# An encoder trunk on one core: the first block's rounding moved to VectorE, the first transfers reordered, fewer warm-up products, second block ordered by operand

## The chip, the cores and the metric

The kernel runs on one core of one Trainium2 chip. The metric is the device time of one execution in microseconds (us), as the median of several runs. One further execution was recorded by the hardware profiler; every row below comes from that one. PE is TensorE, PEld its weight loads, DVE is VectorE, ACT is ScalarE, POOL is GpSimd and SP is SyncE, which here only starts transfers.

## The reference, cut to what matters

Two layers work on a sequence of 512 tokens with 1024 features, all in float32. Each layer adds a token mixer (in layer 0 a short gated convolution, in layer 1 a two-dimensional neighbourhood attention) and then a squared-ReLU MLP to `x`. Only the very first steps are touched by the change:

```python
h = rmsnorm(x, norm_mix[0])
u = h @ conv_w_in[0]          # 1024 x 3072
gate_b, gate_c, v = jnp.split(u, 3, axis=-1)
```

where `rmsnorm(x, g) = x * rsqrt(mean(x*x) + eps) * g`. The kernel multiplies `x` by the gain `g` before the product and by the reciprocal root after it, so the product can start before any mean is known.

## The kernel before, in words

**Precision.** Every float32 operand is split in two parts of a reduced format (float32r): a high part, which is the value rounded, and a low part, which is the value less the high part. A product is then three matmuls that add into the same PSUM bank: high times high, high times low and low times high. For `x` the high part is `a_h` and the low part `a_l`; for weights these are `wave_h` and `wave_l`, views of `w_h` and `w_l`.

**The start.** `x` lies transposed (features on partitions) and comes as eight blocks of 128 features by 512 tokens, `xT[:, k, :]`, 256 KB each, a part of the tile `big`. The first wave of weights is the first four units of `conv_w_in` (four slices `s` of 128 output columns), again in eight blocks by feature: `wave[k]` is 256 KB and lands in `raw`. `par` holds the norm gains and the convolution taps, 32 KB.

- SP starts `par` (L568), then in turn `x[0]`, `x[1]`, `wave[1]`, `x[2]`, `wave[2]` and so on (L570, L572), then four transfers of `x` in token order (`xs`, L574) and the ring of later weights (L592). All of it is one queue, q1.
- ACT starts `wave[0]` itself (L1319), on its own queue q10. It then loads its function table (L1321), rounds `wave[0]` into `wave_h` (L1323, semaphore `piece_hi`), waits for `par`, and rounds in turn `x[k]` times its gain into `a_h` (L1327, semaphore `a_hi`) and `wave[k]` into `wave_h` (L1330).
- DVE waits for `par`, subtracts to get `wave_l` of block 0 (L1824, `piece_split`), and then in turn makes `a_l` (L1828, `a_ready`) and `wave_l` (L1836) of each block.
- PE first runs eight float32 warm-up products of 128 columns on constants (L996); each shows as two passes. POOL makes those constants. Then come the twelve matmuls of block 0, ordered by operand: four slices of high times high (L1001), four of `wave_l` (L1004), four of `a_l` (L1007), each group behind its own semaphore. For blocks 1 to 7 PE waits for `a_ready` and `piece_split` (from block 4 on `w_split`) of that block and runs the twelve matmuls slice by slice through the helper `three` (L769, L770, L771).

After block 7 the remaining units of `conv_w_in` follow, 24 matmuls each. From unit 8 on PE waits for `taken`: DVE must have taken the result of eight units earlier out of its bank (L1819), for which it needs the reciprocal root, computed by ACT and DVE from `xs` and spread over the partitions by two transfers that POOL starts. All later stages (the rest of the convolution, both MLPs, the attention, the final norm) are untouched.

Of the kernel before, what the change touches and what calls it, by code (L numbers as in the profile page):

```python
# [7 lines left out]
KT = D // P  # L8
# [110 lines left out]
def part_end(s, name):  # L119

    return MATRIX[s][0] + 2 * MATRIX[s][1].index(name) + 2
# [99 lines left out]
def encoder(nc, x, x_tok, wave, weights, blocks, sevens, small, gains, rpb, out):  # L221
    f32, f32r = mybir.dt.float32, mybir.dt.float32r
    ALU, ACT = mybir.AluOpType, mybir.ActivationFunctionType
    ctx = ExitStack()
    with ctx:
# [3 lines left out]
        def sem(name):  # L229
            return ctx.enter_context(nc.semaphore(name))  # L230

        xs = sb("xs", [P, 4, D])
        a_h = sb("a_h", [P, KT, SEQ], f32r)
        a_l = sb("a_l", [P, KT, SEQ], f32r)
# [7 lines left out]
        par = sb("par", [P, 8 * KT])  # L242
# [8 lines left out]
        wave_h = wh_all.rearrange("p s (k n) -> p s k n", k=KT)  # L251
        wave_l = wl_all.rearrange("p s (k n) -> p s k n", k=KT)

        def stage(k):
            return raw_all[:, 4 * P * k:4 * P * (k + 1)].rearrange("p (s n) -> p s n", s=4)
# [39 lines left out]
        xT = hraw  # L295
# [71 lines left out]
        bank = [banks[:, 512 * b:512 * b + 512] for b in range(8)]  # L367
# [47 lines left out]
        first_in = [sem(f"first_in{k}") for k in range(KT)]  # L415
        x_in = [sem(f"x_in{m}") for m in range(KT)]
        xs_in = sem("xs_in")
        par_in = sem("par_in")
# [18 lines left out]
        piece_hi = sem("piece_hi")  # L437
        piece_split = sem("piece_split")
        half_hi = sem("half_hi")
        wave_done = sem("wave_done")  # L440
        w_hi = sem("w_hi")
# [10 lines left out]
        rstd_out = sem("rstd_out")  # L452
        rstd_in = sem("rstd_in")
        a_hi = sem("a_hi")
        a_ready = sem("a_ready")

        h_ready = sem("h_ready")
# [62 lines left out]
        def gain(n, m):  # L520
            return par[:, n * KT + m:n * KT + m + 1]
# [43 lines left out]

        @block.sync
        def _(sp):
            sp.dma_start(par[:], small).then_inc(par_in, 16)  # L568
            for k in range(KT):
                sp.dma_start(xT[:, k, :], x[k]).then_inc(x_in[k], 16)  # L570
                if k:
                    sp.dma_start(raw_all[:, 4 * P * k:4 * P * (k + 1)], wave[k]).then_inc(first_in[k], 16)  # L572
            for t in range(4):
                sp.dma_start(xs[:, t, :], x_tok[t]).then_inc(xs_in, 16)  # L574

            plain = [w for w in UNIT_OF_RING if part_of(w) is None]

            def ring_source(r):

                w = UNIT_OF_RING[r]  # L580
                if part_of(w) is None:
                    return weights[plain.index(w)]
                i, part, u = part_of(w)
                at = slice(D * u, D * u + D)
                return sevens[i, Y_ROLES.index(part)][:, at] if part in Y_ROLES else t_dram[i][int(part[1]) - 1][:, at]

            def load_ring(first, last):
                for r in range(first, last):
                    sp.wait_ge(w_split, UNIT_OF_RING[r - 4] + 1)
                    if UNIT_OF_RING[r] in (W_V, W_WO):  # L590
                        sp.wait_ge(t_made[0 if UNIT_OF_RING[r] == W_V else 1], 16 * 4)
                    sp.dma_start(raw_all[:, D * (r % 4):D * (r % 4 + 1)], ring_source(r)).then_inc(raw_in[r % 4], 16)  # L592

            def load_matrix(q, roles=LOAD_ORDER):

                before = {at: role for role, at in ROOMS[q - 1].items()}
                for role in roles:
                    was = before[ROOMS[q][role]]
                    if q == SEQ_ATTN:
                        sp.wait_ge(pv_done, 2 * KT)  # L600
                        sp.wait_ge(s_lo["S4"], 2)
                    elif was != "free":
                        sp.wait_ge(w_split, part_end(q - 1, LAST_USE[was]))
                    elif q in (2, SEQ_ATTN + 1):
                        sp.wait_ge(x_lo, 19 * by_unit(1 if q == 2 else CHUNKS + 1) + 16)
                    else:
                        sp.wait_ge(w_split, part_end(q - 2, "P4"))
                    if was == "T2" and q != SEQ_ATTN:
                        sp.wait_ge(t3_in, 16 * q)
                        sp.wait_ge(t4_in, 16 * q)  # L610
                    sp.dma_start(room[ROOMS[q][role]], blocks[q, Y_ROLES.index(role)]).then_inc(y_in[role], 16)

            load_ring(4, W_OUT + 4)
            load_matrix(1)
            load_ring(W_OUT + 4, W_OUT + 8)
            for q in range(2, SEQ_ATTN):
                load_matrix(q)
            sp.wait_ge(unit_done, MATRIX[SEQ_ATTN - 1][0])
            ends = [ring_of(W_MLP1) + i for i in (-2, 0, 1, 3, 8)]
            load_ring(W_OUT + 8, ends[0])  # L620
            for i, role in enumerate(LOAD_ORDER):
                load_matrix(SEQ_ATTN, (role,))
                load_ring(ends[i], ends[i + 1])
            for q in range(SEQ_ATTN + 1, N_MATRIX):
                load_matrix(q)
            sp.wait_ge(out_act, 1)
            sp.dma_start(out[1], xn[1]).then_inc(stored, 16)
            sp.wait_ge(out_act, 2)
            sp.dma_start(out[0], xn[0]).then_inc(stored, 16)
            sp.wait_ge(out_act, 3)  # L630
            sp.dma_start(out[2][:, 512:D], xn[2][:, 512:D]).then_inc(stored, 16)
            for t in (2, 3):
                sp.wait_ge(out_ready, t - 1)
                sp.dma_start(out[t][:, 0:512], xn[t][:, 0:512]).then_inc(stored, 16)
            sp.wait_ge(stored, 16 * 5)
# [130 lines left out]
        def _(pe):  # L766
# [225 lines left out]
                        last.then_inc(unit_done, 1)  # L992

            pe.wait_ge(const_ready, 3)
            for _ in range(8):
                nc.tensor.matmul(bank[5][:, 0:P], ones[:], ident[:], start=True, stop=True)  # L996

            pe.wait_ge(piece_hi, 1)
            pe.wait_ge(a_hi, 1)
            for s in range(4):  # L1000
                nc.tensor.matmul(bank[s][:], wave_h[:, s, 0, :], a_h[:, 0, :], start=True, stop=False)  # L1001
            pe.wait_ge(piece_split, 1)
# [2 lines left out]
            pe.wait_ge(a_ready, 1)  # L1005
            for s in range(4):
                nc.tensor.matmul(bank[s][:], wave_h[:, s, 0, :], a_l[:, 0, :], start=False, stop=False)  # L1007
            for k in range(1, KT):
                pe.wait_ge(a_ready, k + 1)
                if k < 4:  # L1010
                    pe.wait_ge(piece_split, k + 1)
                else:
                    pe.wait_ge(w_split, k - 3)
                for s in range(4):
                    last = three(bank[s][:], wave_h[:, s, k, :], wave_l[:, s, k, :], a_h[:, k, :], a_l[:, k, :],
                                 False, k == KT - 1)
                    if k == KT - 1:
                        last.then_inc(unit_done, 1)
                if k == 4:
                    last.then_inc(wave_done, 1)  # L1020
# [87 lines left out]
        def _(act):  # L1108
# [208 lines left out]
                    second(tc + c)  # L1317

            act.dma_start(raw_all[:, 0:4 * P], wave[0]).then_inc(first_in[0], 16)  # L1319
            act.wait_ge(const_ready, 1)  # L1320
            nc.scalar.activation(tok[:, 4, :], ones[:, 0:4], ACT.Sqrt)  # L1321
            act.wait_ge(first_in[0], 16)
            nc.scalar.activation(wave_h[:, :, 0, :], stage(0), ACT.Copy).then_inc(piece_hi, 1)  # L1323
            act.wait_ge(par_in, 16)
            for k in range(KT):
                act.wait_ge(x_in[k], 16)
                nc.scalar.activation(a_h[:, k, :], xT[:, k, :], ACT.Copy, scale=gain(0, k)).then_inc(a_hi, 1)  # L1327
                if k:
                    act.wait_ge(first_in[k], 16)
                    nc.scalar.activation(wave_h[:, :, k, :], stage(k), ACT.Copy).then_inc(piece_hi if k < 4 else w_hi, 1)  # L1330

            act.wait_ge(xs_in, 16 * 4)
            for t in range(4):
# [159 lines left out]
        def _(dve):  # L1493
# [323 lines left out]
            def scaled(w, b, dst):  # L1817
# [1 line left out]
                nc.vector.tensor_tensor(dst, bank[b][:], rstd, ALU.mult).then_inc(taken, 1)  # L1819

            dve.wait_ge(par_in, 16)

            dve.wait_ge(piece_hi, 1)
            nc.vector.tensor_tensor(wave_l[:, :, 0, :], stage(0), wave_h[:, :, 0, :].bitcast(f32), ALU.subtract  # L1824
                                    ).then_inc(piece_split, 1)
            for k in range(KT):
                dve.wait_ge(a_hi, k + 1)
                nc.vector.scalar_tensor_tensor(out=a_l[:, k, :], in0=xT[:, k, :], scalar=gain(0, k),  # L1828
                                               in1=a_h[:, k, :].bitcast(f32), op0=ALU.mult,
                                               op1=ALU.subtract).then_inc(a_ready, 1)  # L1830
                if k:
                    if k < 4:
                        dve.wait_ge(piece_hi, k + 1)
                    else:
                        dve.wait_ge(w_hi, k - 3)
                    nc.vector.tensor_tensor(wave_l[:, :, k, :], stage(k), wave_h[:, :, k, :].bitcast(f32), ALU.subtract  # L1836
                                            ).then_inc(piece_split if k < 4 else w_split, 1)
# [348 lines left out]
```

## Time and profile before

| | us |
|---|---|
| median of three runs | 1039.65 |
| lowest and highest of them | 1038.97, 1040.02 |
| the profiled execution, its own time | 1039.44 |
| its span, first to last instruction | 1037.3 |
| PE busy in it | 1028.6 (99%) |
| DVE, ACT, POOL busy | 842.0 (81%), 599.2 (58%), 105.1 (10%) |

The span leaves 2.1 us of the execution's time outside the first and last instruction. Times of rows are from the start of the span. In a timeline row the columns are start, duration, engine, line, operation, what is written and read with its shape, and the number of instructions merged; in brackets stands the idle time of that engine before it and what ended it. A matmul's duration is longer than the distance between two of them, since they are pipelined, and their ends are modelled.

### The profile page before, as it was taken

What the parts mean: (1) busy time and instruction counts of PE and PEld (TensorE: products, weight loads), DVE (VectorE), ACT (ScalarE), POOL (GpSimd) and SP (SyncE); (2) the same over time, 40 slices, a digit from 0 to 9 for tenths busy, and PEclk for the clock granted to TensorE, in tenths of its full rate; (3) what the DMA queues carried; (4) which work ended last, traced back from release to release, by engine and by line L of the source; (5) the groups of instructions that cost most, each with busy time, mean ns of one, the idle gap of its engine ahead of it and who ended that gap; (6) DMA issues with size and microseconds to landing.
All of it is one profiled execution on the core that took longest, in us unless ns stands there. A gap on an engine that the chain in (4) does not pass through costs nothing.

```text
span 1037.3 us, 15366 instructions
## 1 busy us (share of the span) xinstructions
PE 1028.6 (99%) x6088; PEld 903.3 (87%) x6088; DVE 842.0 (81%) x1173; ACT 599.2 (58%) x837; POOL 105.1 (10%) x160
## 2 busy tenths in 40 slices
PE   9999999999999999999999999999999999999997
PEld 7888888988998998998888888889888988988985
DVE  4497788699899689688997667797899798698697
ACT  6221356565584574575775555656664774674675
POOL 0347101000000000001013000000000000000003
PEclk9999999999999999999999999999999999999999
DMA  8798979226745645633998733166056547447423
GB/s 325 141 397 288 292 204 251 84 50 224 205 131 163 186 130 172 175 99 97 372 263 238 212 106 111 43 213 253 1 127 208 163 133 202 149 134 202 148 51 112
DMA packets 37110, 182.97 MB, mean 176 GB/s; under 512 B 5808, under 2 KB 5936, under 8 KB 22960
## 3 DMA queue, kind: packets, MB, share of 16 engines
q1 hardware_dynamic: 23184, 108.57, 29.8%
q0 software_dynamic: 13568, 72.91, 28.4%
q8 instruction: 48, 0.79, 0.3%
q10 hardware_dynamic: 288, 0.52, 0.2%
q14 instruction: 22, 0.18, 0.1%
HBM read 137.20 MB, written 27.33 MB: 159 GB/s over the span
## 4 chain that ended last, share of the span: by engine, by line
PE 95%; DVE 3%; DMA 1%; ACT 1%; issue 0%; POOL 0%; POOLq 0%; ACTq 0%; DVEq 0%
PE bank L769 30%; PE bank L770 30%; PE bank L771 30%; PE bank L974 2%; PE bank L952 1%; PE bank L937 1%; DVE w_l L1508 1%; DMA raw<-weights 1%; PE bank L792 1%; DVE big L1947 0%; PE bank L996 0%; DVE hx L1953 0%; DVE a_l L1721 0%; ACT big L1167 0%; ACT big L1144 0%
## 5 line engine op out<-in xcount | busy, mean ns | idle before, releaser
L1116 ACT ACTIVATE w_h<-big 128x1024 fp32r<-128x1024 f32 x210 | 221.7, 1058 | 216.2 <-PE bank L771 215.5
L769 PE MATMUL bank<-a_h,w_h 128*128 128x256 f32 (+1 forms) x892 | 294.4, 330 | 0.3 <-DVE w_l L1508 0.3
L771 PE MATMUL bank<-a_h,w_l 128*128 128x256 f32 (+1 forms) x892 | 292.8, 328 | 0.0
L770 PE MATMUL bank<-a_l,w_h 128*128 128x256 f32 (+1 forms) x892 | 292.8, 328 | 0.0
L1508 DVE TENSOR_TENSOR w_l<-big,w_h 128x1024 fp32r<-128x1024 f32 x210 | 252.1, 1227 | 21.8 <-ACT w_h L1116 21.8
L769 PE MATMUL bank<-w_h,hx 128*128 128x512 f32 x568 | 221.8, 391 | 0.0
L770 PE MATMUL bank<-w_l,hx 128*128 128x512 f32 x568 | 221.1, 389 | 0.0
L771 PE MATMUL bank<-w_h,hx 128*128 128x512 f32 x568 | 221.0, 389 | 0.0
L769 PEld LDWEIGHTS bank<-a_h,w_h 128*128 128x128 f32 x892 | 169.6, 190 | 16.0 <-issue 0.5
L771 PEld LDWEIGHTS bank<-a_h,w_l 128*128 128x128 f32 x892 | 169.6, 190 | 15.0
L770 PEld LDWEIGHTS bank<-a_l,w_h 128*128 128x128 f32 x892 | 169.6, 190 | 14.4
L1116 ACT ACTIVATE w_h<-raw 128x1024 fp32r<-128x1024 f32 x79 | 83.2, 1057 | 84.6 <-PE bank L771 52.6
L769 PEld LDWEIGHTS bank<-w_h,hx 128*128 128x128 f32 x568 | 106.6, 188 | 22.7 <-issue 0.8
L771 PEld LDWEIGHTS bank<-w_h,hx 128*128 128x128 f32 x568 | 106.6, 188 | 22.3
L770 PEld LDWEIGHTS bank<-w_l,hx 128*128 128x128 f32 x568 | 106.7, 188 | 21.6
L1508 DVE TENSOR_TENSOR w_l<-raw,w_h 128x1024 fp32r<-128x1024 f32 x79 | 95.5, 1217 | 4.8 <-ACT w_h L1116 4.7
L769 PE MATMUL bank<-sx,w_h 128*128 128x256 f32 x288 | 81.5, 283 | 0.0
L770 PE MATMUL bank<-sx,w_h 128*128 128x256 f32 x288 | 81.5, 283 | 0.0
L771 PE MATMUL bank<-sx,w_l 128*128 128x256 f32 x288 | 81.5, 283 | 0.0
L644 POOL DMA_DIRECT2D big<-big x15 | 13.0, 866 | 516.1 <-DVE w_l L1508 516.1
L1670 DVE TENSOR_TENSOR xs<-bank,xs 128x1024 f32<-128x1024 f32 x36 | 43.9, 1219 | 15.0 <-issue 13.1
L769 PEld LDWEIGHTS bank<-sx,w_h 128*128 128x128 f32 x288 | 55.3, 192 | 0.0
(189 smaller groups left out, 1243.3 us busy)
## 6 DMA issues: line engine op xcount, KB each, us to landing
big<-blocks SPq DMA_DIRECT2D x56, 1024.0 KB, 5.0
big<-big POOLq DMA_DIRECT2D x30, 1024.0 KB, 7.7
raw<-weights SPq DMA_DIRECT2D x52, 512.0 KB, 8.5
raw<-t_sums SPq DMA_DIRECT2D x16, 512.0 KB, 3.6
t_sums<-sevens POOLq DMA_DIRECT2D x6, 1024.0 KB, 13.7
t_sums<-t_sums POOLq DMA_DIRECT2D x6, 1024.0 KB, 12.5
raw<-sevens SPq DMA_DIRECT2D x12, 512.0 KB, 7.0
bias_tiles<-big POOLq DMA_DIRECT2D x8, 632.0 KB, 9.8
```

Of the source, the lines that this page charges most:

```text
L644: pool.dma_start(room[at["Y11"]], room[at["T2"]], accum_op=ALU.add).then_inc(t3_in, 16)
L769: nc.tensor.matmul(dst, sh, mh, start=start, stop=False, skip_group_check=again)
L770: nc.tensor.matmul(dst, sh, ml, start=False, stop=False, skip_group_check=again)
L771: return nc.tensor.matmul(dst, sl, mh, start=False, stop=stop, skip_group_check=again)
L792: last = nc.tensor.transpose(bank[b][:, at:at + P], xn[2 * half + t][:, P * k:P * k + P], ident[:])
L937: last = nc.tensor.matmul(score[half][par_][:, score_at(half, n)], q[rows, P * b:P * b + P], k[rows, keys], start=q is q_h and k is k_h, s ...
L952: last = nc.tensor.transpose(tposed[par_][0:width, P * t:P * t + P], prob[half][:, at + P * c:at + P * c + width], ident[:])
L974: last = nc.tensor.matmul(dst[rows, P * b:P * b + P], V_AT[b][c][:, feats], probT[half][:, at:at + P], start=c == 0, stop=c == 1)
L1116: nc.scalar.activation(wh_all[:, w % SLOTS, :], src, ACT.Copy).then_inc(w_hi, 1)
L1508: nc.vector.tensor_tensor(wl_all[:, s, :], src, wh_all[:, s, :].bitcast(f32), ALU.subtract).then_inc(w_split, 1)
L1670: nc.vector.tensor_tensor(dst, src, dst, ALU.add).then_inc(adds, 2)
```

## The change

VectorE instead of ScalarE rounds block 0 of `x` into `a_h`, as soon as `par` and `x[0]` are there, with a semaphore of its own. SP starts with `x[0]`; `par` is started by ACT, behind `wave[0]` on q10. There are six warm-up products instead of eight. Block 1 gets an order by operand like that of block 0, here with `a_l` before `wave_l`, each group behind its own wait. ACT's counts of `a_hi` stay what they were: block 1 now counts two.

```diff
+        first_hi = sem("first_hi")
...
         def _(sp):
-            sp.dma_start(par[:], small).then_inc(par_in, 16)
             for k in range(KT):
                 sp.dma_start(xT[:, k, :], x[k]).then_inc(x_in[k], 16)
...
             pe.wait_ge(const_ready, 3)
-            for _ in range(8):
+            for _ in range(6):
                 nc.tensor.matmul(bank[5][:, 0:P], ones[:], ident[:], start=True, stop=True)
 
             pe.wait_ge(piece_hi, 1)
-            pe.wait_ge(a_hi, 1)
+            pe.wait_ge(first_hi, 1)
...
-            for k in range(1, KT):
+            pe.wait_ge(piece_hi, 2)
+            pe.wait_ge(a_hi, 2)
+            for s in range(4):
+                nc.tensor.matmul(bank[s][:], wave_h[:, s, 1, :], a_h[:, 1, :], start=False, stop=False)
+            pe.wait_ge(a_ready, 2)
+            for s in range(4):
+                nc.tensor.matmul(bank[s][:], wave_h[:, s, 1, :], a_l[:, 1, :], start=False, stop=False)
+            pe.wait_ge(piece_split, 2)
+            for s in range(4):
+                nc.tensor.matmul(bank[s][:], wave_l[:, s, 1, :], a_h[:, 1, :], start=False, stop=False)
+            for k in range(2, KT):
                 pe.wait_ge(a_ready, k + 1)
...
             act.dma_start(raw_all[:, 0:4 * P], wave[0]).then_inc(first_in[0], 16)
+            act.dma_start(par[:], small).then_inc(par_in, 16)
...
-            for k in range(KT):
+            for k in range(1, KT):
                 act.wait_ge(x_in[k], 16)
-                nc.scalar.activation(a_h[:, k, :], xT[:, k, :], ACT.Copy, scale=gain(0, k)).then_inc(a_hi, 1)
-                if k:
-                    act.wait_ge(first_in[k], 16)
-                    nc.scalar.activation(wave_h[:, :, k, :], stage(k), ACT.Copy).then_inc(piece_hi if k < 4 else w_hi, 1)
+                nc.scalar.activation(a_h[:, k, :], xT[:, k, :], ACT.Copy, scale=gain(0, k)).then_inc(a_hi, 2 if k == 1 else 1)
+                act.wait_ge(first_in[k], 16)
+                nc.scalar.activation(wave_h[:, :, k, :], stage(k), ACT.Copy).then_inc(piece_hi if k < 4 else w_hi, 1)
...
             dve.wait_ge(par_in, 16)
-
+            dve.wait_ge(x_in[0], 16)
+            nc.vector.tensor_scalar(a_h[:, 0, :], xT[:, 0, :], gain(0, 0), None, ALU.mult).then_inc(first_hi, 1)
             dve.wait_ge(piece_hi, 1)
...
+            dve.wait_ge(first_hi, 1)
             for k in range(KT):
-                dve.wait_ge(a_hi, k + 1)
+                if k:
+                    dve.wait_ge(a_hi, k + 1)
```

## Rows read from the trace of the kernel before

**Rows 1.** The profile page, part 1: busy time, share of the span, instructions

```profile
PE 1028.6 (99%) x6088; PEld 903.3 (87%) x6088; DVE 842.0 (81%) x1173; ACT 599.2 (58%) x837; POOL 105.1 (10%) x160
```

**Rows 2.** PE's waits over the whole span: us in total, times, longest

```profile
PE bank L996 <- POOL ident L656: 1.7, 1, 1.7
PE bank L769 <- DVE w_l L1508: 0.3, 1, 0.3
```

**Rows 3.** Timeline of PE at the start, from several narrow stretches

```profile
1.67 3.78 PE L996 MATMUL bank<-ident,ones 128*128 128x128 f32 x16 [1.67 <-POOL ident L656]
...
5.03 0.42 PE L996 MATMUL bank<-ident,ones 128*128 128x128 f32 x1
5.29 0.76 PE L1001 MATMUL bank<-a_h,w_h 128*128 128x512 f32 x1
...
5.85 0.90 PE L1001 MATMUL bank<-a_h,w_h 128*128 128x512 f32 x3
...
6.59 1.08 PE L1004 MATMUL bank<-a_h,w_l 128*128 128x512 f32 x4
7.51 1.08 PE L1007 MATMUL bank<-a_l,w_h 128*128 128x512 f32 x4
8.43 0.39 PE L769 MATMUL bank<-a_h,w_h 128*128 128x512 f32 x1
```

**Rows 4.** Timeline of ACT at the start

```profile
0.76 0.40 ACTq L1319 DMA_DIRECT2D raw<-wave  x1
1.19 1.28 ACT L1321 ACT_TABLE_LOAD   x1 [1.19 <-PEq L2179]
...
3.70 0.63 ACT L1323 ACTIVATE w_h<-raw 128x512 fp32r<-128x512 f32 x1 [1.01 <-DMA raw<-wave]
4.42 0.72 ACT L1327 ACTIVATE a_h<-big,par 128x512 fp32r<-128x512 f32 x1
5.76 0.72 ACT L1327 ACTIVATE a_h<-big,par 128x512 fp32r<-128x512 f32 x1 [0.62 <-DMA big<-x]
6.79 0.63 ACT L1330 ACTIVATE w_h<-raw 128x512 fp32r<-128x512 f32 x1 [0.30 <-DMA raw<-wave]
```

**Rows 5.** Weight loads by line: ns min/median/max, first and last start

```profile
L996 PEld LDWEIGHTS bank<-ident,ones x16: 287/333/333, 1.7 to 4.8; 128*128 128x128 f32 x16
...
L1004 PEld LDWEIGHTS bank<-a_h,w_l x4: 187/188/188, 6.4 to 7.0; 128*128 128x128 f32 x4
```

**Rows 6.** Windows: length, busy PE, PEld, DVE, ACT, POOL, granted clock, DMA share, GB/s

```profile
1.67:5.29 3.62, 3.62 (x17) 3.52 (x17) 0.81 (x2) 2.36 (x4) 1.58 (x3) 1.00 0.88 262
```

**Rows 7.** One line of DVE later in the kernel: ns min/median/max, starts, form

```profile
L1871 DVE TENSOR_SCALAR big<-big,par x8: 486/486/603, 46.9 to 95.7; 128x512 f32<-128x512 f32 x8
```

**Rows 8.** Timeline of DVE: blocks 0 and 1, then the first bank taken

```profile
5.18 0.75 DVE L1828 SCALAR_TENSOR_TENSOR a_l<-big,par,a_h 128x512 fp32r<-128x512 f32 x1
...
7.45 0.69 DVE L1836 TENSOR_TENSOR w_l<-raw,w_h 128x512 fp32r<-128x512 f32 x1 [0.18 <-ACT w_h L1330]
...
43.42 1.29 DVE L1819 TENSOR_TENSOR big<-bank,big 128x512 f32<-128x512 f32 x2 [12.44 <-DMA big<-rstd_row]
```

**Rows 9.** Timeline of SP: the issue of `x[0]` and `x[1]`

```profile
1.18 0.90 SPq L570 DMA_DIRECT2D big<-x  x2
```

**Rows 10.** First issues: count, size, us to landing (`x` is `x[0]`, SP's wave is `wave[1]`)

```profile
raw<-wave ACTq DMA_DIRECT2D x1, 256.0 KB, 2.9
big<-x SPq DMA_DIRECT2D x1, 256.0 KB, 3.1
par<-small SPq DMA_DIRECT2D x1, 32.0 KB, 2.3
...
raw<-wave SPq DMA_DIRECT2D x1, 256.0 KB, 4.6
```

**Rows 11.** DMA queues from 2.5 to 3.1 us: packets, MB, share of 16 engines

```profile
q10 hardware_dynamic: 97, 0.18, 79.4%
q1 hardware_dynamic: 28, 0.04, 18.2%
```

## The prediction, made before the changed kernel ran

> **What bounds the kernel now.** I read the page's first part, PE's waits, the timelines of the first 10 us engine by engine, then the transfers. PE is busy 99% of the span [rows 1] and waits twice: 1.7 us at the start for POOL's constants and 0.3 us once far behind [rows 2]. So PE's stream sets the time from its first product on, and what this change can give or take is the moment at which the stream of real products stands where it stood before; the reader may take the 8.43 us at which block 1 begins as the mark [rows 3].
>
> Two things release the first real product at 5.29, and they tie. The sixteen warm-up passes stand (5.03 - 1.67) / 15 = 0.22 us apart, and the last, begun at 5.03, leaves PE at about 5.25. And `a_h` of block 0 ends on ACT at 4.42 + 0.72 = 5.14 [rows 4]; a semaphore needs about 0.1 us. Taking away one alone would give nothing; the change takes both.
>
> The third thing is the clock. A weight load takes 333 ns in the warm-up and 188 ns from 6.4 us on [rows 5], and the first two real products stand 0.56 us apart where later ones stand 0.23, (8.43 - 6.59) / 8 [rows 3]. I read this as the lower of the two levels (1.2 GHz) until about 5.9 us and the higher (2.4 GHz) behind it, after PE had worked without a break from 1.67. The granted-clock column reads 1.00 over the whole of it [rows 6] and does not show the step; the durations do.
>
> **The change, part by part.**
>
> *The transfers.* `x[0]` is issued at about 0.75 instead of 1.18 [rows 9], beside `wave[0]` at 0.76 [rows 4]. Before, `wave[0]` landed at 0.76 + 2.9 = 3.66 and `x[0]` at 1.18 + 3.1 = 4.28 [rows 10]. From 2.5 to 3.1 `wave[0]`'s queue had 79.4% of the engines against 18.2% of the other [rows 11]; now `x[0]` contends from the first packet. So `wave[0]` lands later than 3.66 and `x[0]` earlier than 4.28; the two carry the same bytes, and by 4.28 both had landed with `par` as well, so 4.28 is the upper bound for both. I take 3.95, the middle of the two. `par` comes behind `wave[0]` on q10, with an eighth of its bytes. It cannot land before `wave[0]` (3.66 at the least); behind 3.95 its own share, and `x[1]` contending then, I put at 0.25 (a 256 KB transfer followed another by about 0.6, 4.28 - 3.66, and this is an eighth of one with smaller rows): 4.2, ends 3.7 and 4.6. Alone in front it had taken 2.3 from issue to landing [rows 10], which also gives no more than 1.16 + 2.3 = 3.5 on an empty queue.
>
> The Trainium skill ("DMA: Bandwidth & Descriptors", section "Queues, rings and completion order") says that each DMA engine takes turns packet by packet between the queues that have work for it; by that rule `wave[0]` and `x[0]` would land together near 4 us and `par` would share the engines with `x[1]` rather than follow at once, which speaks against this change. The rows above show such sharing only for the short overlap of the two queues.
>
> *Rounding on DVE.* The nearest row is the same form, one tensor and one column of `par`, 128x512: 486 ns [rows 7]. Above it lies the 0.75 us of the form with a second tensor [rows 8]. Only the output type differs from the first, so I take 0.49: 4.2 + 0.49 = 4.7. ACT's rounding of `wave[0]`, 0.63, ends at 3.95 + 0.05 + 0.63 = 4.63, so `par` decides, narrowly. With 0.12 us to the first product (5.14 to 5.26 to 5.29 before) PE starts at about 4.85, 0.44 us earlier. Ends: with `wave[0]` rounded as early as before, 3.70 + 0.63 + 0.12 = 4.5; and 4.6 + 0.75 + 0.12 = 5.5, which is 0.2 later than now.
>
> *Two warm-up products fewer.* Four passes of 0.22 are 0.88 us: PE is free at about 4.4, before 4.85. The edit is not felt by itself; it opens a break of about 0.5 us in PE's work ahead of the clock's step.
>
> *What an earlier start is worth.* If the clock still rises at about 5.9, the 0.44 us lie at the lower level. A product there takes between 0.41 (an estimate: 0.23 times 333 / 188) and 0.56 us [rows 3, 5], so about one more product is done by 5.9, and one product is worth 0.23 us behind it. The term is **-0.23 us** (with a start at 4.5, two products, -0.45; at 5.5, +0.1; a whole 0.8 only if the clock rose earlier too).
>
> *Work queued behind the new waits.* DVE waits for `x[0]` and `par` and only then makes `wave_l` and `a_l` of block 0: 4.7 + 0.69 = 5.4 and 5.4 + 0.75 = 6.2, against 5.18 + 0.75 = 5.93 before [rows 8]. PE wants them four and eight products after 4.85, at the lower level not before 6.2 and 7.1. Cost 0; with the upper ends, 5.5 + 0.7, it is still covered, since PE then starts later too. ACT's second issue, 0.40 [rows 4], pushes the table load from 1.19 to 1.6 and its end to about 3.1, under the wait for `wave[0]`: 0. ACT has 0.72 less to do before block 1. SP's later transfers are issued 0.43 us earlier, and from `x[1]` on they follow the bandwidth: a gain of 0 to 0.4 in landing, which nobody waits for.
>
> *Block 1 by operand.* Before, `wave_l` of block 1 was ready at 7.45 + 0.69 = 8.14, 0.29 us ahead of the 8.43 at which PE asked for it [rows 3, 8]; PE now asks for the first group at about 8.2, and that needs only `wave_h` (6.79 + 0.63 = 7.42) and `a_h` (5.76 + 0.72 = 6.48) [rows 4]. The old order would have left 0.06 us. The new one has 1.8 us more for `wave_l`. The count of products and weight loads is the same, and block 0 in that order ran at 0.23 as well. Cost 0.
>
> *Later.* PE meets unit 8 at about 8.43 + 84 x 0.23 + 96 x 0.23 = 49.8; DVE takes the first bank from 43.42 on [rows 8], 5 us before. From there on each step hangs on PE's, so the gain is carried to the end, unless the one wait of 0.3 us at L769 [rows 2] grows by as much.
>
> **Sum.** 1039.44 (own time of the profiled execution) - 0.23 = 1039.2. That execution lies 0.21 below the median of the runs, so against the median it would be 1039.4; I name 1039.3. Two tenths of a per cent, 2.1 us, is about what a measurement of this kernel tells from no change; the whole mechanism is a tenth of that.
>
> **Rivals.**
>
> *The clock rises later.* The break of 0.5 us stands where before PE worked without one. If the stay at the lower level starts anew, it lasts again 5.9 - 1.67 = 4.2 us, to about 9.05. In that time 4.2 / 0.56 = 7.5 to 4.2 / 0.41 = 10.2 products are done; before, 12 + 0.62 / 0.23 = 14.7 were done by 9.05. The lack of 4.5 to 7.2 products costs 1.0 to 1.65 us: **1040.5 to 1041.1**, slower than before. Each us at the lower level costs about half a us, so it passes 2.1 us of loss only if the clock stays low to about (2.1 + 0.23) / 0.5 = 4.7 us behind 5.9, 10.6. For it: the break is new, and the step came only after work without one. Against it: the break is short beside 4.2 us, and PE works again well before 5.9. The Trainium skill ("TensorE: Matmul & The Clock Gate", Part 1, "What's actually happening") says that the level follows how busy the engine was recently and that the moment of the step is not tied to the kernel's start but differs from run to run. By that rule the break may cost some executions the step and others not, so a median can show any part of the loss; one trace can't bear it out, though the three runs do lie 1.05 us apart.
>
> *The operand is no earlier.* If `par` or `x[0]` lands at 4.5 or later, PE starts at 5.2 to 5.5 as before: **1039.4 to 1039.6**. For it: `par` now has 256 KB ahead of it and small rows. Against: the engines had moved all three transfers by 4.28.
>
> *The edits do less or more than they say.* The start comes at 4.5 and the clock rises earlier as well, or a later stage gains: 1038.6. Against it: nothing in the rows shows the step of the clock moving forward with less warm-up work.
>
> **How the numbers follow.** The forecast has 0.52 (its own range 1038.8 to 1039.8), the later clock 0.27, of which 0.06 beyond 2.1 us, the operand no earlier 0.15, the larger gain 0.06. Eight in ten reach from 1038.6 to 1041.1: the bounds of the start, a few tenths between executions, and the later clock at its price. Faster by over 0.2% needs 2.1 us, more than PE's whole idle start of 1.67 [rows 2], so 0.02; slower by over 0.2% is the late end of the clock's case, 0.06; the same 0.92.
>
> **What would show it.** In the changed kernel's timeline: the first L1001 product at 4.85 (4.5 to 5.2) instead of 5.29, DVE's new instruction of 0.49 us ending about 0.1 us ahead of it and released by `par`; twelve warm-up passes ending near 4.4; block 1's first product at 8.2 without idle time. The step of the clock is read from the weight loads falling to 188 ns: at 5.9 if I am right; at 8 to 10, with products 0.41 to 0.56 apart until then, if the first rival holds. I am wrong if PE idles between blocks 0 and 2, or if the time moves by more than the start does, which would mean that a later stage reacts.

## The result, and the profile after

The changed kernel takes **1041.78 us** in the median of 22 runs (1039.79 to 1043.37), against 1039.95 for the kernel before in as many runs beside them (1038.97 to 1041.7). The ratio is 1.0017 with a 95% interval of [1.0011, 1.0023]: slower by 0.17%, some 1.8 us. The forecast was 1039.3 with a range to 1041.1, so the time lies above the range. The profiled execution has 1041.34 and a span of 1039.3, 0.4 us below the median; the runs spread over 3.6 us, so what its trace shows is not the loss of every run.

The timeline of PE in the changed kernel, from several narrow stretches, against [rows 3]; L1011 is the first line of block 1, L769 here the first product of block 2:

```profile
3.97 0.63 PE L996 MATMUL bank<-ident,ones 128*128 128x128 f32 x2
...
6.16 0.77 PE L1001 MATMUL bank<-a_h,w_h 128*128 128x512 f32 x1 [1.55 <-DVE a_h L1833]
...
7.58 0.63 PE L1001 MATMUL bank<-a_h,w_h 128*128 128x512 f32 x1
8.00 0.63 PE L1004 MATMUL bank<-a_h,w_l 128*128 128x512 f32 x1
...
9.50 0.40 PE L1007 MATMUL bank<-a_l,w_h 128*128 128x512 f32 x1
...
10.42 0.86 PE L1011 MATMUL bank<-a_h,w_h 128*128 128x512 f32 x3
...
13.16 0.39 PE L769 MATMUL bank<-a_h,w_h 128*128 128x512 f32 x1
```

The first real product starts at 6.16 instead of 5.29: 0.87 us **later**, where 0.44 earlier was forecast. Ahead of it PE is idle for 1.55 us. From there to 9.3 the products stand 0.43 us apart, as 7.58 and 8.00 show. Block 1 begins at 10.42 instead of 8.43, which is 1.99 us: 0.87 from the start, and 1.12 because block 0 takes 10.42 - 6.16 = 4.26 us instead of 3.14. The two spans differ by 2.0 us as well, so nothing behind block 0 adds to it or gives it back.

Two weight loads around the step, of the kernel before and then of the changed kernel, against [rows 5]:

```profile
5.42 0.33 PEld L1001 LDWEIGHTS bank<-a_h,w_h 128*128 128x128 f32 x1
5.85 0.23 PEld L1001 LDWEIGHTS bank<-a_h,w_h 128*128 128x128 f32 x1
...
8.86 0.33 PEld L1004 LDWEIGHTS bank<-a_h,w_l 128*128 128x128 f32 x1
9.27 0.19 PEld L1007 LDWEIGHTS bank<-a_l,w_h 128*128 128x128 f32 x1
```

In the changed kernel the clock is still at the lower level at 8.86 and at the higher at 9.27. Before, the last slow load (333 ns) began at 5.42.

What released the start: the timeline of DVE in the changed kernel, against [rows 8], and that of ACT, against [rows 4].

```profile
5.53 0.49 DVE L1833 TENSOR_SCALAR a_h<-big,par 128x512 fp32r<-128x512 f32 x1 [5.53 <-DMA par<-small]
5.93 0.68 DVE L1835 TENSOR_TENSOR w_l<-raw,w_h 128x512 fp32r<-128x512 f32 x1
```

```profile
1.19 0.45 ACTq L1330 DMA_DIRECT2D par<-small  x1
...
4.58 0.63 ACT L1334 ACTIVATE w_h<-raw 128x512 fp32r<-128x512 f32 x1 [1.41 <-DMA raw<-wave]
```

DVE's rounding costs the 0.49 us that was forecast, but it could begin only at 5.53, released by `par`. ACT's rounding of `wave[0]` began at 4.58 instead of 3.70 and was done at 5.21, so it was not what PE waited for last. But even with `par` there in time, the start would have come no earlier than 5.29: DVE's rounding ends at 5.53 + 0.49 = 6.02, 0.14 us ahead of the first product, and the same behind ACT's 5.21 gives 5.35 (an estimate). The landings of the three transfers, against [rows 10]:

```profile
big<-x SPq DMA_DIRECT2D x1, 256.0 KB, 3.6
raw<-wave ACTq DMA_DIRECT2D x1, 256.0 KB, 3.8
...
par<-small ACTq DMA_DIRECT2D x1, 32.0 KB, 4.3
```

`x[0]` lands at 0.75 + 3.6 = 4.35, `wave[0]` at 0.76 + 3.8 = 4.6, and `par` at 1.19 + 4.3 = 5.5; before, `par` was there at 0.75 + 2.3 = 3.05. `x[0]`, though issued 0.43 us sooner, landed no sooner than the 4.28 of before, and `wave[0]` 0.9 us later than its 3.66. Why `par` is so late is seen in the two queues of the changed kernel, against [rows 11]: from 1.7 to 2.3 us, from 2.3 to 4.0, from 4.0 to 5.0 and over the whole from 1.7 to 5.0 (packets, MB, share of 16 engines):

```profile
q1 hardware_dynamic: 37, 0.08, 82.9%
...
q1 hardware_dynamic: 167, 0.31, 49.5%
q10 hardware_dynamic: 141, 0.25, 49.0%
...
q1 hardware_dynamic: 178, 0.33, 91.0%
q10 hardware_dynamic: 147, 0.04, 17.2%
...
q1 hardware_dynamic: 382, 0.71, 68.1%
q10 hardware_dynamic: 288, 0.30, 30.4%
```

Up to 2.3 us q10 moved nothing: all 37 packets are q1's, although `wave[0]` was issued 0.01 us after `x[0]`. Then the two queues share the engines evenly, 49.5% and 49.0%. While most of `par`'s small packets went through, from 4.0 on, q1 moved 0.33 MB beside q10's 0.04. By 5.0 q1 had passed 0.71 MB, that is `x[0]`, `x[1]` and most of `wave[1]`, before the 0.30 MB of `wave[0]` and `par` were done.

### The profile page after: what moved, and what is told of

The parts are those of the page before. It is cut to its first block, busy times and chain, and to the rows that moved or that the text cites. A ratio compares the mean times of both kernels' runs of the same rounds, so it can differ in the third digit from the quotient of the medians.

```text
span 1039.3 us, 15358 instructions
## 1 busy us (share of the span) xinstructions
PE 1028.9 (99%) x6084; PEld 903.2 (87%) x6084; DVE 841.7 (81%) x1174; ACT 598.1 (58%) x836; POOL 105.0 (10%) x160
## 4 chain that ended last, share of the span: by engine, by line
PE 98%; DMA 0%; DVE 0%; ACT 0%; issue 0%; ACTq 0%; DVEq 0%
PE bank L769 31%; PE bank L770 31%; PE bank L771 31%; PE bank L974 2%; PE bank L952 1%; PE bank L937 1%; PE bank L792 1%; DMA par<-small 0%; PE bank L1001 0%; ACT big L1154 0%; PE bank L1004 0%; DVE xs L1665 0%; PE bank L1011 0%; PE bank L1007 0%; PE bank L1017 0%
## 5 line engine op out<-in xcount | busy, mean ns | idle before, releaser
L769 PE MATMUL bank<-a_h,w_h 128*128 128x256 f32 (+1 forms) x888 | 292.8, 330 | 0.0
L769 PE MATMUL bank<-w_h,hx 128*128 128x512 f32 x568 | 221.8, 391 | 0.0
L769 PEld LDWEIGHTS bank<-a_h,w_h 128*128 128x128 f32 x888 | 168.8, 190 | 15.6 <-issue 0.2
L769 PEld LDWEIGHTS bank<-w_h,hx 128*128 128x128 f32 x568 | 106.6, 188 | 22.8 <-issue 0.8
L769 PE MATMUL bank<-sx,w_h 128*128 128x256 f32 x288 | 81.5, 283 | 0.0
L769 PEld LDWEIGHTS bank<-sx,w_h 128*128 128x128 f32 x288 | 55.3, 192 | 0.0
```

The costliest lines, as they stand in the source:

```text
L769: nc.tensor.matmul(dst, sh, mh, start=start, stop=False, skip_group_check=again)
```

## The experiments

Twelve kernels ran, each in 11 runs, in three groups; each group had 33 runs of the kernel before on the same chip, with medians of 1039.70, 1039.81 and 1039.93. The changed kernel was not in these groups, so it is best compared by the ratios to the kernel before; its own is 1.0017 [1.0011, 1.0023]. The theory: `par` on q10 behind `wave[0]` makes the first operand late, and the longer break that opens between the warm-up and the first product puts the step of the clock off. Names that begin with `b_` are edits of the kernel before, those with `a_` of the changed kernel.

### Norm weights back in front (`a_par_sp`)

```diff
+            sp.dma_start(par[:], small).then_inc(par_in, 16)
             for k in range(KT):
...
-            act.dma_start(par[:], small).then_inc(par_in, 16)
```

> The changed kernel with the norm weights back as SyncE's first transfer; the rest of the change stays. Theory (late norm weights cost 0.9 us, the break the rest): par lands near 3.1, x[0] near 4.3, the first real product starts at 4.9 to 5.1, the break shrinks from 1.6 to about 0.6 us; the median is 0.9 to 1.8 us below the changed kernel. Rival (the queue is not the matter, VectorE's rounding is): no more than 0.3 us below the changed kernel.

Measured: 1039.87 us, ratio to the kernel before 1.0000 [0.9991, 1.0009]; 1.9 us below the changed kernel. DVE and PE in it (line numbers of PE are one higher):

```profile
4.34 0.49 DVE L1833 TENSOR_SCALAR a_h<-big,par 128x512 fp32r<-128x512 f32 x1 [4.34 <-DMA big<-x]
...
4.97 1.70 PE L1002 MATMUL bank<-a_h,w_h 128*128 128x512 f32 x4 [0.36 <-DVE a_h L1833]
...
8.35 1.07 PE L1012 MATMUL bank<-a_h,w_h 128*128 128x512 f32 x4
```

VectorE's rounding now waits for `x[0]`, the first product starts at 4.97, idle time is 0.36 us, and the whole loss is gone. So the rounding on VectorE, the six warm-up products and block 1's order together cost nothing when `par` comes in time. The edit also puts `x[0]` back to second place; `b_par_act` and `a_par_second` below look at the two moves apart. And no gain from the earlier start is seen: the median is that of the kernel before, and in the traces a start 0.32 us earlier than 5.29 gave block 1 at 8.35, 0.08 earlier than 8.43, with the last slow load at 5.96 instead of 5.42.

### The move of the norm weights alone (`b_par_act`)

```diff
-            sp.dma_start(par[:], small).then_inc(par_in, 16)
...
             act.dma_start(raw_all[:, 0:4 * P], wave[0]).then_inc(first_in[0], 16)
+            act.dma_start(par[:], small).then_inc(par_in, 16)
```

> The kernel before with the one move of the norm weights to ScalarE's queue behind the first weights; eight warm-up products, ScalarE rounds block 0. Theory: wave[0] lands near 4.5 and par near 5.5, ScalarE ends a_h of block 0 at about 6.3 and PE starts at 6.4, 1.1 us later than before, behind a break of about 1.1 us: median 1.0 to 2.0 us above the kernel before. Rival (the move is harmless and the loss comes from the other edits): within 0.3 us of the kernel before.

Measured: 1042.20 us, ratio 1.0022 [1.0013, 1.0031], 2.5 us above the kernel before, more than expected. DVE and PE (its lines are one lower):

```profile
5.96 0.69 DVE L1824 TENSOR_TENSOR w_l<-raw,w_h 128x512 fp32r<-128x512 f32 x1 [5.96 <-DMA par<-small]
...
6.83 2.05 PE L1000 MATMUL bank<-a_h,w_h 128*128 128x512 f32 x4 [1.37 <-ACT a_h L1327]
...
10.98 0.40 PE L768 MATMUL bank<-a_h,w_h 128*128 128x512 f32 x1
```

`par` lands at 5.96 here, PE starts at 6.83 and block 1 at 10.98. This one edit, which leaves `x[0]` in front on q1, is enough for the whole loss (the intervals of the two kernels overlap). Its start lies 0.67 us behind the changed kernel's 6.16; 0.43 of that is `par`, later in this execution, and 0.23 the rounding, 0.72 on ScalarE against 0.49 on VectorE.

### Norm weights second, behind `x[0]` (`a_par_second`)

```diff
             for k in range(KT):
                 sp.dma_start(xT[:, k, :], x[k]).then_inc(x_in[k], 16)
+                if k == 0:
+                    sp.dma_start(par[:], small).then_inc(par_in, 16)
...
-            act.dma_start(par[:], small).then_inc(par_in, 16)
```

> The changed kernel with the norm weights on SyncE's queue right behind x[0], ahead of x[1]; x[0] is still first. Theory (par is late because its small rows come last of all and x[1] shares the engines): par lands near 4.4 to 4.6, x[0] near 4.3, but wave[0] still near 4.5, since x[0] contends with it; PE starts at about 5.3 behind ScalarE's rounding of wave[0] (4.6 + 0.63), block 1 at 8.4 to 10 by the clock; median between the kernel before and 1.7 us above it, at least 0.3 us below the changed kernel. Rival (only par's place matters): PE starts at 5.0 and the median is that of the variant with par first.

Measured: 1040.53 us, ratio 1.0009 [1.0000, 1.0018]; `par` landed at 4.3, `wave[0]` at 4.15, the first product at 4.98.

```profile
4.35 0.48 DVE L1834 TENSOR_SCALAR a_h<-big,par 128x512 fp32r<-128x512 f32 x1 [4.35 <-DMA par<-small]
...
4.98 1.98 PE L1003 MATMUL bank<-a_h,w_h 128*128 128x512 f32 x4 [0.37 <-DVE a_h L1834]
```

The start is the rival's 4.98: `x[0]` in front is not what makes it late, and behind `x[0]` on q1 `par` comes 1.2 us sooner than behind `wave[0]` on q10. My detail about `wave[0]` was wrong; it came at 4.15, between 3.66 and 4.6. The median lies between the two kernels, as the theory had it, and its interval reaches to no change; whether `x[0]` in front has a price of its own is open.

### The break alone (`b_warm6`, `b_warm7`, `b_warm0`)

```diff
-            for _ in range(8):
+            for _ in range(6):
                 nc.tensor.matmul(bank[5][:, 0:P], ones[:], ident[:], start=True, stop=True)
```

This is `b_warm6`; `b_warm7` has seven of these products and `b_warm0` none.

> The kernel before, with six warm-up products instead of eight and nothing else. The start of the first real product is set by a_h of block 0 (end 5.14 before), so it stays at about 5.3 and a break of about 0.9 us opens behind the twelfth pass. Theory (the break ahead of the clock's step costs time): weight loads stay at 333 ns well behind 5.9 us in some or all executions, block 1 begins up to 1.5 us later than 8.43, and the median is 0.4 to 1.5 us above the kernel before. Rival (only the moment of the first product counts, the break does not): block 1 at 8.4, median within 0.2 us of the kernel before.

> The kernel before with seven warm-up products: passes end near 4.8, the first real product at 5.3, so a break between none (eight products) and the 0.70 us of idle time of six. Theory (the loss hangs on the length of the break): idle 0.25 to 0.3 us, median 0 to 0.8 us above the kernel before, so between eight and six. Rival (the loss hangs on whether there is any break): like six products, 1.4 to 1.7 us above.

> The kernel before without any warm-up product. It prices the clock alone: the first real product stays at about 5.3 us, since a_h of block 0 sets it. Theory (the stay at the lower level begins anew with the first real product): products stand 0.43 us apart from 5.3 on until 8 to 9.5 us, block 1 begins 1.5 to 2 us later than 8.43, and the median is 1.5 to 2.1 us above the kernel before, no worse than six warm-up products by more than 0.5 us. Rival (the twelve passes of six warm-up products count for most of what sixteen count): at least 1 us slower than with six.

Measured: six products 1041.41 us, ratio 1.0010 [1.0001, 1.0019]; seven 1039.61, ratio 0.9998 [0.9989, 1.0007]; none 1041.40, ratio 1.0013 [1.0005, 1.0022]. PE with six, then with seven:

```profile
5.30 2.04 PE L1001 MATMUL bank<-a_h,w_h 128*128 128x512 f32 x4 [0.70 <-ACT a_h L1327]
...
8.85 1.52 PE L1007 MATMUL bank<-a_l,w_h 128*128 128x512 f32 x4
10.21 0.39 PE L769 MATMUL bank<-a_h,w_h 128*128 128x512 f32 x1
```

```profile
5.21 2.03 PE L1001 MATMUL bank<-a_h,w_h 128*128 128x512 f32 x4 [0.18 <-ACT a_h L1327]
...
8.90 0.39 PE L769 MATMUL bank<-a_h,w_h 128*128 128x512 f32 x1
```

With six the first product starts at 5.30 as before, and still block 1 begins at 10.21, 1.78 us later than 8.43 and a little more than expected. Only the last four passes are gone, with 0.70 us of idle time in their place. It is not the number of passes alone: `a_par_sp` has the same twelve, with 0.36 us of idle time, and lost nothing. So a break of 0.70 us ahead of the step moves the step of the clock even with `par` in time, and its price in the median is that of having no warm-up at all: 1.7 us with six products, 1.6 with none. With 0.18 us of idle time no loss shows, and the median lies 0.3 us below that of the kernel before, just under the theory's range. The price is not paid in every execution: of the eleven runs with six products four lie at 1038.67 to 1039.76 and seven at 1041.4 to 1042.04, with nothing between; the one with the trace, 1041.52, is of the seven. Without any warm-up none of the eleven lies below 1040.31.

### The break filled, `par` still late (`a_warm11`, `a_warm14`)

```diff
-            for _ in range(6):
+            for _ in range(11):
                 nc.tensor.matmul(bank[5][:, 0:P], ones[:], ident[:], start=True, stop=True)
```

This is `a_warm11`; `a_warm14` has fourteen.

> The changed kernel with eleven warm-up products instead of six, so that PE works from 1.67 to about 6.4 us, past the late first operand. Theory (the break holds the clock down): the clock has risen before the first real product, which starts at 6.3 to 6.5; twelve products at 0.23 us give block 1 at about 9.1 instead of 10.42; the median is 0.8 to 1.4 us below the changed kernel though five products were added. Rival (the late operand alone sets the loss): the start and so the time is the same or up to 0.3 us later.

> The changed kernel with fourteen warm-up products. At the lower level 28 passes reach from 1.67 to 7.7 us, at the higher from about 5.9 on they end near 6.8, so there is no break ahead of the first product whenever the clock rises; norm weights stay late. Theory (with unbroken work the clock is up before the first real product in every execution): first product at 6.4 to 7.7, block 1 at 9.1 to 10.4, and the runs lie closer together than those of the changed kernel (2 us instead of 3.6); median 0.2 to 1.2 us below the changed kernel. Rival (work on constants does not keep or raise the clock in most executions, so eleven products gained little for that): median at or above that of eleven products (1041.4), runs spread over 3 us.

Measured: eleven 1041.38 us (1039.89 to 1042.54), ratio 1.0012 [1.0004, 1.0021]; fourteen 1041.35 (1040.28 to 1043.10), ratio 1.0012 [1.0003, 1.0021]. Both medians are 0.4 us below the changed kernel's, but the intervals overlap with its own, so the filled break shows no clear gain; 0.8 to 1.4 us had been expected from eleven. PE with eleven, then with fourteen:

```profile
6.17 1.17 PE L1001 MATMUL bank<-a_h,w_h 128*128 128x512 f32 x4 [0.35 <-DVE a_h L1833]
...
8.99 1.07 PE L1011 MATMUL bank<-a_h,w_h 128*128 128x512 f32 x4
```

```profile
1.67 6.25 PE L996 MATMUL bank<-ident,ones 128*128 128x128 f32 x28 [1.67 <-POOL ident L656]
7.67 1.17 PE L1001 MATMUL bank<-a_h,w_h 128*128 128x512 f32 x4
...
10.49 0.39 PE L1011 MATMUL bank<-a_h,w_h 128*128 128x512 f32 x1
```

The profiled execution with eleven did what the theory says: the start as late as in the changed kernel (6.17), the clock up before it, block 1 at 8.99 instead of 10.42. But it is the fastest of its eleven runs, 1039.89, so this is not the common case. The execution with fourteen, the slowest of its runs at 1043.10, shows one way to lose it: its 28 passes went by at (7.67 - 1.67) / 28 = 0.21 us all the way, so the clock was still low at 7.4 us after work without a break from 1.67. There the warm-up itself held the first product up, since VectorE's rounding had ended at 6.08 + 0.49 = 6.57. The step came at different moments in the two traces, and more warm-up behind a late operand does not buy it reliably. On medians this pair speaks rather against the theory than for it: with no break or a short one, medians of 1.4 to 1.7 us above the kernel before stay. So that the break is what costs the changed kernel its second part is argued from the traces and from `b_warm6`, not shown.

### An earlier warm-up, and the best guess (`a_par_sp_ones9`, `b_ones10`, `a_par_sp_warm7`)

```diff
-            pe.wait_ge(const_ready, 3)
-            for _ in range(8):
-                nc.tensor.matmul(bank[5][:, 0:P], ones[:], ident[:], start=True, stop=True)
+            pe.wait_ge(const_ready, 1)
+            for _ in range(10):
+                nc.tensor.matmul(bank[5][:, 0:P], ones[:], ones[:], start=True, stop=True)
```

This is `b_ones10`; `a_par_sp_ones9` has the same edit with nine on top of `a_par_sp`, and `a_par_sp_warm7` is `a_par_sp` with seven of the old products.

> The kernel before with ten warm-up products on the tile of ones alone, from about 1.0 to 5.25 us; nothing else changes, the first real product stays at 5.3. Theory: the clock rises about 0.65 us earlier, ahead of the first real product; block 1 at 8.1, median 0.2 to 0.5 us below the kernel before. Rival (the constants' values or the start do not matter to the step): no change within 0.15 us.

> The changed kernel with the norm weights first on SyncE's queue again and nine warm-up products that multiply the tile of ones by itself, so that PE waits for the first constant only. Theory (the step of the clock follows unbroken work): warm-up from about 1.0 to 4.85 us, the first real product at 4.95 behind next to no break, the clock up by about 5.3; block 1 at 7.8 to 8.0, median 0.3 to 0.8 us below the kernel before. Rival (the step does not move with the start of the warm-up): median within 0.2 us of the kernel before.

> The changed kernel with the norm weights first on SyncE's queue again and seven warm-up products: the best guess at a version that keeps VectorE's rounding. Theory: par at 3.1, x[0] at 4.3, first product at 4.95 with passes ending near 4.8, so no idle time; block 1 at 8.2; median 0.1 to 0.4 us below the kernel before. Rival (an earlier start is spent at the lower clock and is worth nothing): within 0.1 us of the kernel before.

Measured: 1039.86 us, ratio 1.0000 [0.9991, 1.0009]; 1039.95, ratio 1.0002 [0.9993, 1.0011]; 1039.97, ratio 1.0000 [0.9991, 1.0009]. All three theories fell and all three rivals held: none is faster than the kernel before. PE of `b_ones10`:

```profile
1.01 4.64 PE L996 MATMUL bank<-ones 128*128 128x128 f32 x20 [1.01 <-POOL ones L653]
5.30 2.00 PE L1001 MATMUL bank<-a_h,w_h 128*128 128x512 f32 x4
...
8.95 0.39 PE L769 MATMUL bank<-a_h,w_h 128*128 128x512 f32 x1
```

The warm-up began 0.66 us earlier, but in this execution the last slow weight load was at 6.72 and block 1 came at 8.95, later than 8.43. Work begun earlier, on a tile of ones, did not bring the step forward, and the median shows no gain either. The version that keeps VectorE's rounding with seven products started at 5.20 (`x[0]` landed at 4.57 in that execution) and is as fast as the kernel before, not faster.

### Block 1 slice by slice (`a_slices`)

```diff
-            pe.wait_ge(piece_hi, 2)
-            pe.wait_ge(a_hi, 2)
...
-            for k in range(2, KT):
+            for k in range(1, KT):
```

> The changed kernel with block 1 slice by slice as before; all other edits stay. Theory (the order by operand costs and brings nothing while PE is late): start 6.2, block 1 takes 2.7 us behind the step of the clock, no idle time; median within 0.4 us of the changed kernel's 1041.8. Rival (the change of bank at every product costs TensorE time, or the new order hides a wait): 0.3 us or more faster, or 0.3 us of idle time ahead of block 1.

Measured: 1042.12 us, ratio 1.0018 [1.0010, 1.0027], the same as the changed kernel's 1.0017. There is no idle time ahead of block 1, and its twelve products take 13.41 - 10.68 = 2.73 us, in the new order 13.16 - 10.42 = 2.74. The order by operand neither costs nor hides anything here, while PE is late.

### All executions side by side

From the profiled execution of each kernel, in us: idle time of PE ahead of the first real product, its start, the start of the last weight load of over 250 ns (that is, the clock still low), the start of block 2, the span, and the span less block 2's start.

| kernel | idle | first product | last slow load | block 2 | span | rest |
|---|---|---|---|---|---|---|
| a_warm11 | 0.35 | 6.17 | 4.40 | 11.71 | 1037.8 | 1026.1 |
| before | 0 | 5.29 | 5.42 | 11.18 | 1037.3 | 1026.1 |
| a_par_sp_warm7 | 0.17 | 5.20 | 5.76 | 11.16 | 1038.0 | 1026.8 |
| a_par_sp | 0.36 | 4.97 | 5.96 | 11.07 | 1037.2 | 1026.1 |
| a_par_sp_ones9 | 0 | 5.03 | 6.02 | 11.26 | 1037.8 | 1026.5 |
| a_par_second | 0.37 | 4.98 | 6.40 | 11.35 | 1037.8 | 1026.5 |
| b_warm7 | 0.18 | 5.21 | 6.62 | 11.64 | 1037.7 | 1026.1 |
| b_ones10 | 0 | 5.30 | 6.72 | 11.67 | 1037.9 | 1026.2 |
| a_warm14 | 0 | 7.67 | 7.39 | 13.21 | 1041.0 | 1027.8 |
| **after** | 1.55 | 6.16 | 8.86 | 13.16 | 1039.3 | 1026.1 |
| a_slices | 1.76 | 6.36 | 9.06 | 13.41 | 1040.3 | 1026.9 |
| b_warm6 | 0.70 | 5.30 | 9.28 | 12.93 | 1039.4 | 1026.5 |
| b_par_act | 1.37 | 6.83 | 9.53 | 13.72 | 1040.5 | 1026.8 |
| b_warm0 | no warm-up | 5.07 | 10.76 | 13.35 | 1039.6 | 1026.2 |

Two things are to be seen, from one execution of each kernel. Where PE had 0.37 us of idle time or less, the clock had risen by 7.8; where it had 0.70 or more, or no warm-up, not before 8.8. And the rest of the kernel takes 1026.1 to 1026.9 in thirteen of the fourteen, with no order in it by what happened at the start (in the fourteenth PE waits 0.9 us at L952 and 0.4 at L769 later on): but for some 0.8 us, the time is decided in the first 13 us.

## Why the prediction was wrong

**What failed: the landing of `par`.** The step put `par` 0.25 us behind `wave[0]`, at 4.2 with ends of 3.7 and 4.6. Measured were 5.5 in the changed kernel, 5.5, 5.7, 6.0 and 6.1 in the four other kernels that have `par` on q10. The upper end was off by 0.9 us and more. I had reasoned from totals, that the engines had moved `wave[0]`, `x[0]` and `par` by 4.28 in the old order and so would in the new; that bound fell for all three, with `x[0]` at 4.35 and `wave[0]` at 4.6 against the 3.95 that I took. But SP does not stop behind `x[0]`; `x[1]` and `wave[1]` follow on q1, and 0.71 MB went past q10's 0.30. The mechanism stood in the prediction without a price. The trace shows even shares of the engines, 49.5% and 49.0%, from 2.3 to 4.0 us, and 178 packets of q1 beside 147 of q10 from 4.0 to 5.0. By the Trainium skill ("DMA: Bandwidth & Descriptors", section "Queues, rings and completion order") each engine takes turns packet by packet between the queues with work, and the trace agrees with it in these shares. A price could have been had from the rows of before, as an estimate: with turns like those that the trace now shows, the 128 rows of `par` go beside as many packets of q1, of 0.18 MB / 97 = 1.9 KB each [rows 11], 0.27 MB in all, which at 262 GB/s [rows 6] takes 1 us; behind 4.28 that is a landing at 5.3.

**The start** came therefore at 6.16, outside its ends of 4.5 and 5.5. With `par` in front (`a_par_sp`) it came at 4.97, 0.12 from the 4.85 forecast, and block 1 at 8.35 against 8.2; but that is luck in part, since `x[0]` at 4.34 released it there and not `par`.

**The rivals were taken one at a time.** "The clock rises later" was priced at 1.0 to 1.65 us with the first product at 4.85, "the operand is no earlier" at no change. In the trace they come together: the later operand makes the break 1.55 us long instead of the forecast 0.5, the step comes late as well, and the sum is 0.87 + 1.12 = 1.99 us. That the break puts the step off is shown for the kernel before (`b_warm6`); in the changed kernel it is argued, since filling the break gave no clear gain. The size of the clock's price was near: 1.12 here, 1.7 in the median of six products, 1.6 in that of none. That its step came at 8.9 to 9.3, inside the 8 to 10 named for it, is luck. The rival let the stay at the lower level begin anew with the first product and last 4.2 us; counted from the first product, the last slow load began 2.7 us later in the changed kernel and in `b_par_act`, 4.0 in `b_warm6` and 5.7 in `b_warm0`. From 6.16 on, 4.2 us would have reached to 10.4.

**What was right.** DVE's instruction, 0.49 us. The warm-up ending near 4.4 (the last passes, from 3.97 on, end at 4.6). No wait for the work queued behind DVE's new waits: `wave_l` at 5.93 + 0.68 = 6.6 and PE asked for it at 8.0. Block 1's order at 0 (`a_slices`). Nothing later reacts: the rest of the changed kernel equals that of the kernel before in the table. An earlier start is worth little: 0.23 us was forecast, and `a_par_sp` shows no gain that its interval can tell from none. Of the two releasers that tie, one was taken away alone, two warm-up products in `b_warm6`, and the start stayed at 5.30 as forecast; the earlier rounding with all eight products was not run. But with six products the break that it opens costs 1.7 us; the sentence that fewer warm-up products are "not felt" held only up to the break, which the first rival then took up.

**The moment of the step.** With the warm-up begun at 1.67 or 1.68 and a break of 0.37 us at most, the last slow load began anywhere from 4.40 to 7.39 in the table. This agrees with the Trainium skill ("TensorE: Matmul & The Clock Gate", Part 1, "What's actually happening"), by which the step is not tied to the kernel's start and differs from run to run. The two groups of runs with six products point the same way, though only one of those runs has a trace.

**Left open.** How the loss of the changed kernel divides between the late operand and the clock in the runs that have no trace; why eleven products bring back so little in the median, since only the fastest of their runs has a trace; and what a break between 0.37 and 0.70 us would cost, since no kernel had one.

## What to carry to other kernels

A small operand that everything waits for belongs at the head of a queue: there its 32 KB landed 2.1 to 2.7 us behind their issue, behind 256 KB on a second queue 4.3 to 4.9. Its place on a second queue is priced by what both queues move until it is through, not by its own bytes. Idle time of TensorE ahead of the clock's first rise is not free although nothing waits in it: 0.70 us of it cost 1.7 us in the median, about as much as no warm-up at all, where 0.18 us cost nothing. So a warm-up is sized to end at the first product: well before it leaves a break, and the fourteen products that ran past it held it up. And where two rivals of a forecast hang on one another, their sum needs a row of its own.

## What the runs showed that I had not expected

- Of two transfers issued 0.01 us apart on two queues, the second moved no packet until 2.3 us, 0.6 us behind the first (2.0 to 2.4 us in the other kernels with `x[0]` in front), and q10's 32 KB took 4.3 us from issue to landing, where before 256 KB on the same queue had taken 2.9.
- The clock stayed at the lower level to 7.4 us in an execution whose PE had worked without a break since 1.67, and in another with the same start (`a_warm11`) the last slow load began at 4.40.
- A warm-up from 1.01 us on, on a tile of ones, gave the narrowest runs of all (1039.62 to 1040.36) and no gain.
